# PEER expert layers of a two-layer decoder step: 64 prompt tokens move from the dense experts to the fetched ones

## The reference, cut to what matters

```
def one(xi):                                        # xi: normalised tokens
    q = (xi @ wq).reshape(blk, 8, 2, 128)           # 8 heads, two half keys
    s = einsum('nhcd,hckd->nhck', q, keys)          # 128 keys each
    top_s, top_i = lax.top_k(s, 16)
    cand_s = top_s[..., 0, :, None] + top_s[..., 1, None, :]
    cand_i = top_i[..., 0, :, None] * 128 + top_i[..., 1, None, :]
    sel_s, sel_pos = lax.top_k(cand_s, 16)
    idx = take_along_axis(cand_i, sel_pos)          # 8 x 16 of 16384 experts per token
    gate = softmax(sel_s)
    act = gelu(einsum('nhkd,nd->nhk', u_tab[idx], xi))
    return einsum('nhk,nhkd->nd', gate * act, v_tab[idx])
```

## Time and profile before

| | us |
|---|---|
| three runs, lowest / median / highest | 5384.82 / 5394.23 / 5397.02 |
| profiled execution, its own time | 5385.82 |
| its span, first to last instruction | 5384.1 |
| PE busy in the span | 4557.9 (85%) |
| DVE, POOL, ACT busy | 3352.8, 2260.5, 1357.3 |

### The profile page before, as it was taken

The page is one execution under the profiler, slowest core; times in us unless marked ns, Lnnn a source line. Parts: engine busy times, 40 slices in busy tenths (PEclk is TensorE's granted clock), DMA queues, the critical chain, the costliest instruction groups (busy, mean ns, idle before and its releaser), DMA issues. The chain is left out here.

```text
span 5384.1 us, 61880 instructions
## 1 busy us (share of the span) xinstructions
PE 4557.9 (85%) x22764; PEld 3829.9 (71%) x22764; DVE 3352.8 (62%) x6354; ACT 1357.3 (25%) x2086; POOL 2260.5 (42%) x1308
## 2 busy tenths in 40 slices
PE   3246675999989979999977768879998997999996
PEld 3136564988878868888767548777887886888885
DVE  3993434267976658888632361226788665888873
ACT  1111210123335522222210141103333553222220
POOL 1243002356743336666534011144665332666663
PEclk7678757999999989999988777789999999999998
DMA  1001001256745567777411112115665455777751
GB/s 67 0 0 57 16 18 63 90 169 226 226 160 185 181 228 245 234 242 244 151 56 59 61 58 78 45 50 165 224 225 176 176 190 208 247 244 238 238 181 62
DMA packets 380068, 778.48 MB, mean 145 GB/s; under 512 B 21351, under 2 KB 155303, under 8 KB 374408
## 3 DMA queue, kind: packets, MB, share of 16 engines
q1 hardware_dynamic: 338312, 623.73, 34.8%
q0 software_dynamic: 41472, 151.01, 8.1%
HBM read 628.24 MB, written 146.42 MB: 144 GB/s over the span
## 5 line engine op out<-in xcount | busy, mean ns | idle before, releaser
L183 PE MATMUL p0e_y_ps<-p0e_w,p0e_v_parts 128*128 128x512 f32 x3072 | 701.0, 391 | 26.8 <-POOL p0e_v_parts L166 24.7
L183 PE MATMUL p1e_y_ps<-p1e_w,p1e_v_parts 128*128 128x512 f32 x3072 | 698.7, 390 | 26.9 <-POOL p1e_v_parts L166 25.1
L183 PEld LDWEIGHTS p0e_y_ps<-p0e_w,p0e_v_parts 128*128 128x128 f32 x3072 | 578.8, 189 | 148.7 <-POOL p0e_v_parts L166 24.9
L183 PEld LDWEIGHTS p1e_y_ps<-p1e_w,p1e_v_parts 128*128 128x128 f32 x3072 | 577.6, 188 | 147.7 <-POOL p1e_v_parts L166 25.3
L166 POOL TENSOR_TENSOR p0e_v_parts<-p0e_vt,p0e_v_parts 128x512 fp32r<-128x512 f32 x256 | 395.5, 1545 | 264.9 <-ACT p0e_v_parts L161 261.1
L166 POOL TENSOR_TENSOR p1e_v_parts<-p1e_vt,p1e_v_parts 128x512 fp32r<-128x512 f32 x256 | 395.1, 1544 | 263.5 <-ACT p1e_v_parts L161 259.8
L183 PE MATMUL p0s_s_ps<-p_xn,p0s_u_parts 128*128 128x512 f32 x1920 | 449.5, 395 | 0.0
L183 PE MATMUL p1s_s_ps<-p_xn,p1s_u_parts 128*128 128x512 f32 x1920 | 449.5, 395 | 0.0
L183 PEld LDWEIGHTS p0s_s_ps<-p_xn,p0s_u_parts 128*128 128x128 f32 x1920 | 359.7, 188 | 87.4
L183 PEld LDWEIGHTS p1s_s_ps<-p_xn,p1s_u_parts 128*128 128x128 f32 x1920 | 359.0, 187 | 88.0
L161 ACT ACTIVATE p0e_v_parts<-p0e_vt 128x512 fp32r<-128x512 f32 x256 | 161.8, 633 | 545.7 <-PE p0e_y_ps L183 533.4
(11 more groups left out here) (546 smaller groups left out, 8765.9 us busy)
## 6 DMA issues: line engine op xcount, KB each, us to landing
p0e_vt<-peer_v_dram SPq DMA_DIRECT2D x64, 1024.0 KB, 5.7
p1e_vt<-peer_v_dram SPq DMA_DIRECT2D x64, 1024.0 KB, 5.7
p0s_ut<-peer_ut_dram SPq DMA_DIRECT2D x80, 512.0 KB, 3.4
p1s_ut<-peer_ut_dram SPq DMA_DIRECT2D x80, 512.0 KB, 3.4
gates<-p0g_grid SPq DMA_DIRECT2D x16, 2048.0 KB, 7.4
p0e_acts<-activities SPq DMA_DIRECT2D x32, 1024.0 KB, 7.1
p0e_gt<-gates SPq DMA_DIRECT2D x32, 1024.0 KB, 10.2
gates<-p1g_grid SPq DMA_DIRECT2D x16, 2048.0 KB, 7.4
```

Of the source, the lines that this page charges most:

```text
L183: last = pe.matmul(out(a), weights(wp).bitcast(F32R), moving(xp, a).bitcast(F32R), start=start and m == 0, stop=stop and m == len(PRODUCTS ...
```

## The change

The last 64 prompt tokens are taken out of the dense group. The dense group has 448 tokens (TD), and the fetched group 128 (TG), one token on each partition, with all 128 of its experts, so NG is 128. In words:

- The dense matmuls have 448 moving columns in place of 512, and activities, gates and their stores shrink alike. There are 14 blocks of 32 tokens for the gates in place of 16.
- Keys are spread otherwise: 72 in stage s (16 beside the first tile, 14 beside each other) and 56 in stage g, four in each block of 32 tokens in place of three.
- The 128 fetches of u rows are made by a new class `RowDots`, 40 in stage s (10 per tile after the first) and 88 in stage g, three buffers in each.
- The one-hot rows of stage g are made for seven of eight columns in one DVE instruction and one in another; three of the four are multiplied by their gate on ACT (`gate`).
- In stage e all 32 blocks are summed in PSUM, eight banks for the eight pieces, and DVE adds each piece to `h` once, at the end. There are four fetches of v rows per block in place of two, with four buffers as before. Six buffers hold split v weights in place of four. The two halves needn't be added; the sum is transposed instead.

```diff
-NTB = TP // TB
+TG = P
+TD = T - TG
+NTB = TD // TB
 JB = 4
 NJB = P // JB
 N_KEYS = 128
-KEYS_SELECT, KEYS_GATES = 80, 48
-NG = PH * PK // 2
+KEYS_BY_TILE = (16, 14, 14, 14, 14)
+KEYS_SELECT, KEYS_GATES = 72, 56
+DOTS_BY_TILE = 10
+NG = PH * PK
...
+class RowDots:
+
+
+    RING = 3
+
+    def __init__(self, st, dr, rows, x_rows, row_s, first, count):
+        self.rows, self.x_rows, self.row_s, self.first, self.count = rows, x_rows, row_s, first, count
+        self.src = dr["peer_u_rows"]
+        self.fetched = st.sb("fetched", [P, self.RING, D])
+        self.u_got = [st.sem(f"u_got{k}") for k in range(self.RING)]
+        self.dotted = st.sem("dotted")
+
+    def fetch(self, pool, n):
+        if n >= self.count:
+            return
+        g = self.first + n
+        if n >= self.RING:
+            pool.wait_ge(self.dotted, n - self.RING + 1)
+        pool.indirect_dma_start(self.fetched[:, n % self.RING, :], None, self.src,
+                                bass.IndirectOffsetOnAxis(ap=self.rows[:, g:g + 1], axis=0))\
+            .then_inc(self.u_got[n % self.RING], 16)
+
+    def dot(self, dve, n):
+        if n >= self.count:
+            return
+        g, row = self.first + n, self.fetched[:, n % self.RING, :]
+        dve.wait_ge(self.u_got[n % self.RING], 16 * (n // self.RING + 1))
+        dve.tensor_tensor_reduce(row, row, self.x_rows, 1.0, 0.0, ALU.mult, ALU.add, self.row_s[:, g:g + 1])\
+           .then_inc(self.dotted, 1)
...
-                    if n >= KT:
-                        fetch(n - KT)
+                    if n == starts[1]:
+                        pool.wait_ge(rows_ready, 1)
+                    while n >= starts[1] and fetched * (KEYS_SELECT - starts[1]) < dots.count * (n + 1 - starts[1]):
+                        dots.fetch(pool, fetched)
+                        fetched += 1
...
-                        if n % 8 == 7 and n < NQ - 1:
+                        if n == NQ // 2:
                             dot(o, 0)
                     last.then_inc(sc_read, 1)
                     dot(o, 1)
                     dve.drain()
                     for n in range(NQ):
                         dve.max(top[:, n, 8:16], work[:, n, :])
-                    dot(o, 2)
                     dve.drain()
                     for n in range(NQ):
                         dve.max_index(topi[:, n, 8:16], top[:, n, 8:16], work[:, n, :])
-                    dot(o, 3)
+                    dot(o, 2)
...
+        first_dot = DOTS_BY_TILE * (NT - 1)
+        dots = RowDots(st, dr, rows["u"], x_rows, row_s, first_dot, NG - first_dot)
...
-                        for w in range(4):
-                            at_w = slice(4 * r + w, 4 * r + w + 1)
-                            dve.tensor_scalar(one_i[:, r % DEPTH, w, :], cst["iota"], cols[:, k, 0, at_w],
-                                              cols[:, k, 2, at_w], ALU.is_equal, ALU.mult)
-                        dve.tensor_tensor(one_j[:, r % DEPTH, :, :], cst["iota"].unsqueeze(1).to_broadcast([P, 4, P]),
-                                          cols[:, k, 1, 4 * r:4 * r + 4].unsqueeze(2).to_broadcast([P, 4, P]),
-                                          ALU.is_equal).then_inc(hot_ready, 1)
+                        each = cols[:, k, r, :, :].rearrange("p c w -> p (c w)")
+                        t = tb * TB + 4 * r
+                        dve.tensor_tensor(hot[:, r % DEPTH, 1:8, :], cst["iota"].unsqueeze(1).to_broadcast([P, 7, P]),
+                                          each[:, 1:8].unsqueeze(2).to_broadcast([P, 7, P]), ALU.is_equal)
+                        dve.tensor_scalar(gated[:, r % DEPTH, 0, :], cst["iota"], each[:, 0:1],
+                                          sel[:, 2, t:t + 1], ALU.is_equal, ALU.mult).then_inc(hot_ready, 1)
+                        while done * NN < dots.count * (n + 1):
+                            dots.dot(dve, done)
+                            done += 1
...
+                    while done * KEYS_GATES < dots.count * (n + 1):
+                        dots.fetch(pool, done)
+                        done += 1
...
+                def gate(n):
+                    if n >= NN:
+                        return
+                    act.wait_ge(hot_ready, n + 1)
+                    for w in range(1, 4):
+                        t = 4 * n + w
+                        last = act.activation(gated[:, n % DEPTH, w, :], hot[:, n % DEPTH, w, :], ACT.Copy,
+                                              scale=sel[:, 2, t:t + 1])
+                    last.then_inc(gated_ready, 1)
+
                 acts.high(act, 0)
                 acts.high(act, 1)
+                gate(0)
+                gate(1)
                 for tb in range(NTB):
                     k = tb % 2
                     for r in range(NQ4):
+                        n = tb * NQ4 + r
                         if r in AT:
-                            n = tb * KB + AT.index(r)
-                            acts.high(act, n + 2)
-                            acts.gelu(act, n)
+                            acts.high(act, tb * KB + AT.index(r) + 2)
                         if r == 0 and tb >= 2:
                             act.wait_ge(grid_out[k], 16 * (tb // 2))
-                        act.wait_ge(multiplied, tb * NQ4 + r + 1)
+                        act.wait_ge(multiplied, n + 1)
                         act.activation(grid[:, k, :, 4 * r:4 * r + 4].rearrange("p j w -> p w j"), gp[:, r % 2, :, :],
                                        ACT.Copy).then_inc(taken, 1)
+                        gate(n + 2)
+                        if r in AT:
+                            acts.gelu(act, tb * KB + AT.index(r))
...
-        VR, YB = 4, 4
+        VR = 6
...
-                        if m >= YB:
-                            pe.wait_ge(y_added, m - YB + 1)
                         for j in range(JB):
                             if c == 0:
                                 pe.wait_ge(w_ready, n * JB + j + 1)
                             last = multiply_split(
-                                pe, lambda a: y_ps[:, m % YB, :],
+                                pe, lambda a: y_ps[:, c, 0:TD],
                                 lambda part: v_part(m, part)[:, j, :],
-                                lambda part, a: w[:, n % 2, part, j, :], 1, j == 0, j == JB - 1)
+                                lambda part, a: w[:, n % 2, part, j, :], 1, n == 0 and j == 0, n == NJB - 1 and j == JB - 1)
                         last.then_inc(y_ready, 1)
                 pe.wait_ge(summed_all, 1)
+                pe.wait_ge(y_added, 2)
...
+                        if n >= 2:
+                            dve.wait_ge(y_ready, (n - 1) * DC)
...
-                    for c in range(DC):
-                        add(n * DC + c)
-                        if c < JB:
-                            if n + 1 < NJB:
-                                weigh(n + 1, c)
-                        elif c % 2 == 1 and n:
-                            accumulate((n - 1) * GB + (c - JB) // 2)
-                        dve.drain()
+                    for j in range(JB):
+                        if n + 1 < NJB:
+                            weigh(n + 1, j)
+                            dve.drain()
+                        if n:
+                            accumulate((n - 1) * GB + j)
+                            dve.drain()
...
+                for c in range(DC):
+                    add(c)
+                dve.drain()
+                dve.wait_ge(turned_all, 1)
+                dst = h[:, :, TD:T]
+                dve.tensor_tensor(dst, dst, turned, ALU.add)
```

More of the change, by code:

```diff
@@ L1317, in select_experts @@
         acts = Activities(st, dr, layer, xn, 0, KEYS_SELECT, 4, 3, 3)
+        dots = RowDots(st, dr, rows["u"], x_rows, row_s, 0, DOTS_BY_TILE * (NT - 1))
         tr = st.ps("tr", [P, 3, P])
         keys_in = st.sem("keys_in")
-        padded = st.sem("padded")
         staged = st.sem("staged")
@@ L1532, in tile @@
                         dve.drain()
-                        for r in range(2):
-                            dve.tensor_copy(row_gate[r * 64:(r + 1) * 64, :], half(2, r))
+                        dve.tensor_copy(row_gate[:], flat(2))
                         dve.drain()
@@ L1556, in list_rows @@
                     dve.tensor_copy(rows["u"][:], rowf[:, 0, :]).then_inc(rows_ready, 1)
-                    for r in range(2):
-                        some = slice(r * 64, (r + 1) * 64)
-                        dve.tensor_tensor(rowf[some, 1, :], rowf[some, 1, :], half(1, r), ALU.add)
+                    dve.tensor_tensor(rowf[:, 1, :], rowf[:, 1, :], flat(1), ALU.add)
                     dve.tensor_copy(rowf[:, 2, :], row_j[:])
@@ L1569, in _, with spread_gates @@
                     tile(o)
-def spread_gates(nc, dr, cst, layer, nm, sel, xn):
+def spread_gates(nc, dr, cst, layer, nm, sel, xn, rows, x_rows, row_s):
     NQ4 = TB // 4
@@ L1625, in _ @@
                         for w in range(4):
```

(2 more changed lines are left out.)

148 lines of the change are left out of this document (61 added, 87 removed).

## The result

The changed kernel takes 5474.42 us (median of 4 runs, 5468.57 to 5475.8) against 5392.66 us before (4 runs): ratio 1.0151, 95% interval 1.0134 to 1.0169. It is slower, by 82 us, where the prediction had 5140, which is faster by 254. Its profiled execution took 5475.8 us, 90.0 over the one of before.

The account below looks back on a forecast made before the run. PE was taken as the bound in stages s, g and e. Terms -87 + 18 - 52 - 6 = -127 us a layer, -254 in both, took the profiled 5385.8 to 5132, median 5140; own range 5090 to 5200 (45%).

Parts of the forecast that it names:

- Price of a matmul: Dense matmuls on PE: 448 columns cost 200.0 ns, each losing 26.7 ns against 512 columns.
- stage s: Stage s: 72 keys of 4.96 us replace 80 of 5.60, -90.9 us; with waits for DVE, -87 a layer.
- the +4: Stage s: DVE and PE tie, so the last tile may end late; +4 us taken, between 0 and 15.
- Stage g: Stage g: waits for fetches make a key 7.4 us, 414 in all, +18 us a layer; ends -26 and +77.
- the ring: Stage g: ACT, DVE, fetch and POOL wait on each other in a circle over two keys, 14.8 us with a 6.9 landing.
- PE's clock: Stage g: should stay near 1.00; if stalls lowered it, 0.64 us of each key would be lost again.
- Stage e: Stage e: cheaper matmuls save 81.9 us, a stall costs 28; -52 a layer taken, ends -82 and 0.
- The later fetches: Stage e: they meet a wait every 4.8 us, but DVE needs only 4.3, so it is hidden by half a microsecond.
- The stall at the third piece: Stage e: a path of 5.7 us against 4.8 makes PE wait 0.9 us in about 31 blocks, +28 us.
- The end of stage e: After e's last piece: about 3 us remain where 9.1 were needed, -6 us a layer.
- Stage e's DVE and POOL hold each other: Rival, 9%: in e each cast waits 1.25 us, a block needs 21.6 us, e gains -6, kernel 5232.
- The sum: Whole kernel: -87 + 18 - 52 - 6 = -127 us a layer, -254 in both.

Follow-up runs that it names:

- e_ring8: Changed kernel with eight fetch buffers in stage e instead of four: 5237.44 us, ratio to before 0.9709.
- e_none: Changed kernel with stage e fetching and accumulating no row at all: 5151.72 us, one run.
- e_act_cast: Changed kernel with eight fetch buffers in e and the cast of weighed activations on ACT instead of DVE: 5172.93 us, ratio to before 0.9608.
- e_act_ring4: Changed kernel with the cast of weighed activations in e on ACT instead of DVE, still four fetch buffers: 5278.08 us, ratio to before 0.9802.

## Why the prediction was wrong, point by point

**Price of a matmul, stage s.** Right in the main: s gained 82 and 77 us where -87 was forecast. A key takes 4.85 us in s (median of ACT's gelus), 0.11 less than the 4.96 of the sum, and twelve matmuls of e take 2.43 without rows, against 2.40. DVE and PE do tie, as the text said, and the +4 for it was too small: PE waits 9.2 us for DVE between the tiles and 11.4 for the last one,

```profile
1448.98 0.88 PE L1440 MATMUL p0s_tr<-ident,p0s_res 128*128 128x128 f32 x3 [11.42 <-DVEq L1551]
```

where it had waited 1.8 and 4.8 before. That is 14 us more in the first layer, near the bound of 15. With 72 keys of 4.85 the sum would be -98.8 + 14 = -85, against -82 measured; the cheap key and the small +4 made up for each other in part.

**Stage g.** The mechanism was right, shown by fetches issued ahead (-120 us in the kernel) and by no rows at all (-129), and the size was off: +36 and +38 where +18 stood, inside its ends of -26 and +77. With the landing of 7.1 in place of 6.9 the sum would have been 7.5 us a key, +24. Two other parts of the ring were taken too short. ACT's three gates take 0.99 us, not 0.8, and DVE's one-hot row meets POOL's split:

```profile
1708.36 2.59 POOL L170 TENSOR_TENSOR p0g_u_parts<-p0g_ut,p0g_u_parts 128x1024 fp32r<-128x1024 f32 x1 [2.50 <-ACT p0g_u_parts L165]
1708.64 2.40 DVE L1620 TENSOR_SCALAR p0g_gated<-iota,p0g_cols,p_sel 128x128 f32<-128x128 f32 x1
...
1711.07 0.99 ACT L1658 ACTIVATE p0g_gated<-p0g_hot,p_sel 128x128 f32<-128x128 f32 x3 [0.79 <-DVE p0g_gated L1620]
```

2.40 us where 0.26 was counted. Of the 111 one-hot rows of this kind in the window of g, the 25 that began while a split ran took 2.3 us or more, and the 86 others 0.3. And PE's clock, which the text had named as a danger, fell with the stalls: it stood at 0.95, and the same 2240 matmuls were busy for 398.01 us, against 374.05 at 1.00. How the missing 12 us split between these was not measured apart.

**Stage e.** This is the step that failed: "The later fetches meet the same wait every 4.8 us, while DVE needs 1.72 + 1.28 = 3.0 and the wait for POOL that stretches a cast from 0.43 to as much as 1.68, 4.3: hidden, by half a microsecond." It made the chain of DVE's instructions alone. In the trace POOL's are in it too, because the fetch waits for the accumulation and the subtraction for the splits: 1.28 of accumulation, 0.28 until POOL starts, 1.27 of fetch, 2.57 of splits, 0.50 of the subtraction's end and 0.08, 5.98 together. Three such intervals and the one of 6.80 make 24.65 us, and the trace has 24.7 from block to block on average, 742 us for 30 blocks. The rest of the 794 are 33 us up to the first accumulation and 19 behind the last whole block.

The stall at the third piece that the forecast did have was mis-sized besides: its path took 7.47 us instead of 5.7, above all because the product of the first weighing was held (2.05 us for 0.62), and PE stalled 1.95 us in 30 blocks, 58 us where +28 stood. The 75 later waits, 48 us, stood at nothing. What remains when PE is alone was low too: 630 to 643 measured where 614 stood. (The terms -82 and +28 make -54; the text took -52.)

**The end of stage e.** -6 forecast, about -4 measured.

**The rival that came closest.** "Stage e's DVE and POOL hold each other" (9%) named the mechanism and priced it at 21.6 us a block; it was 24.8. Two things were missed. It let a cast wait for one split of 1.25 us, but POOL, late itself behind its fetch, makes two in one go, so a whole 2.55 us come on top. And it took the accumulations of the earlier trace rows as evidence against holding, because none was stretched. They do meet splits, in the kernel before:

```profile
2319.06 1.28 DVE L1795 SCALAR_TENSOR_TENSOR p0e_total<-p0e_fetched,p0e_row_w,p0e_total 128x1024 f32<-128x1024 f32 x1
2319.16 2.32 POOL L166 TENSOR_TENSOR p0e_v_parts<-p0e_vt,p0e_v_parts 128x512 fp32r<-128x512 f32 x1 [1.43 <-ACT p0e_v_parts L161]
```

About every second accumulation starts like this one, 0.10 us ahead of a split and with POOL idle. It keeps its length, and the split is the one held, 2.32 us instead of 1.29. So the starting order decides who waits.

The Trainium skill (SBUF — State Buffer, SBUF: two separate sides) states that a DVE instruction with two SBUF inputs and a GpSimd instruction that reads SBUF exclude each other by a lock that the first to start holds for its whole instruction. The two rows above agree. The held subtraction and accumulation (3.35 and 3.68 us) seem not to, since they have the earlier start in the records, by 0.31 and 0.04 us, and waited for two splits. But POOL was not idle then: its fetch was in its last 0.3 us (2303.82 + 1.27 = 2305.09, with the subtraction from 2304.80), and the splits followed at once. In the first layer's e of six traces (before, after, `e_ring8`, `e_none`, `e_act_cast`, `e_act_ring4`), 396 DVE instructions started with POOL idle and a split starting within their own length, and none was held; of 262 that started in the last 0.35 us of a fetch with a split right behind it, 257 were. Why two splits in a row pass is not shown.

**The sum.** -127 a layer was forecast and +41 and +48 came. Of the difference of some 171, e makes 143 (+91 for -52), g 19, s 8 and the end 2. What is shown: the ring in e (buffers 237 us in the kernel), DVE's load (cast on ACT, a further 65) and the ring in g (fetches ahead, 120).

## What to carry to other kernels

When a ring of buffers keeps its size and its traffic doubles, write down the whole circle that one buffer closes, through every engine's queue, and count in it what the waiting instruction holds up behind it; on this kernel four more buffers (16 KB a partition) took 237 us off. An engine that is late catches up with its instructions back to back, and another engine's instruction can then wait for all of them, as DVE's did for two splits of POOL, so a half-microsecond margin there is no cover. That an instruction was never stretched does not show that it cannot be: look at who started first. Here an indirect fetch had to be issued several uses ahead of its consumer (120 us in g), and on the consumer's schedule, not spread evenly over time (65 us in s with 8 dots).

## What was not expected of the hardware

- DVE stood still behind two POOL splits in a row: 3.35 us for a subtraction of 0.62, 3.68 for an accumulation of 1.28, when it started in the last 0.3 us of a POOL fetch that the splits followed. The splits kept their own length, 1.27 each. With POOL idle at its start, an accumulation was not held, and the split waited instead (2.32 us for 1.29).
- A DVE instruction with a single wide input, of 128 elements, was held as well: 2.40 us instead of 0.33, beside a split of 2.59. The kernel before has such rows too, up to 2.57 us (L1604).
- Fetches landed later in g than in s, and later still with fetches ahead: a median of 6.2 us in s (193 GB/s), 7.1 in g (261 GB/s) and 8.2 in g with fetches ahead (300 GB/s). Traffic alone does not explain it: in e of the changed kernel the median is 4.7 us at 238 GB/s, where it was 6.6 before at 233.
